# A gated linear attention and RWKV-7 layer in two phases: the second phase's four instruction lists in another order

## The chip, the cores and the metric

One core of one Trainium2 chip runs one program. The metric is the time of one execution in microseconds on the device; three executions were timed and the median counts.

## The reference, cut to what matters

One layer reads 4096 prompt tokens (one stream) and 128 sample tokens (8 streams of 16 tokens, with states carried in). Its mixer has two head groups. The first, gated linear attention, is the kernel's first phase. The second, RWKV-7, is its second phase, together with the output projection:

```
h = rms_norm(x, norm_pre);  p = h @ w_in
xm = p_shift + rwkv_mu * (prev - p_shift)          # prev: the row of the token before
r, kr, vr, wd, ad = split(xm)                      # 512, 512, 512, 64, 64 columns
w = exp(-0.6065 * sigmoid(w0 + tanh(wd) @ w_up))   # decay, low rank
a = sigmoid(a0 + ad @ a_up)                        # rate, low rank
kk = kr * k_k / norm(kr * k_k);  kr = kr * (1 + (a - 1) * k_a)
S_t = S_{t-1} (diag(w_t) - kk_t^T (a_t * kk_t)) + v_t^T k_t ;  y_t = S_t r_t     # 8 heads of 64
y = group_norm(y) * ln_w + ln_b                    # mean and variance over the 64 of a head
o_rwkv = (y + sum(r * kr * r_k) * vr) * silu(z_r)
x = x + rms_norm([o_gla, o_rwkv] @ w_out, norm_post)
```

All of it is float32. The order of the work does not enter into it.

## The kernel before, in words

**Blocks, tiles and chunks.** Block 0 holds the 128 sample tokens, and blocks 1 to 16 hold 256 prompt tokens each. A block is cut in tiles of 128 tokens (two of them, block 0 has one) for everything after the recurrence, and in chunks of 64 tokens (four of them, block 0 has two) for the recurrence. Within a chunk the recurrence is solved by a triangular inverse, so the state is only touched once in a chunk.

**The lists.** In the second phase each engine has one list for a *body*, which is one pass over a block: `PE_BODY` (TensorE), `ACT_BODY` (ScalarE), `DVE_BODY` (VectorE), `POOL_BODY` (GpSimd) and `SP_BODY` (the queue that issues DMAs). `body_jobs` goes through a list from left to right for b = 0 to 17 and hands out jobs; each engine runs its own jobs strictly in that order. Between engines there are only semaphores. A word is a job, its number after the colon is a chunk or a tile, `*3` is three times, and a dash in front means the block before. `out` marks a point; at the points of the last bodies the jobs of the output projection are put in.

**Three streams run in one body.** For block b+2 the projection is made: 39 *pieces* on TensorE, `x12` three times and `x4`, `x6`, `x0`, `x2`, `x8`, `x10` six times each, every piece 8 matmuls of 128x256. After a round, ScalarE (`taken`, L2028 and L2031) and VectorE (`mixed`, L2265 and L2271) make the token shift. The low-rank rounds are `lwa0` and `lwa2` (L1744, `rank`); ScalarE takes them with `tanh` (L2054), and VectorE makes the running decay from both halves of `lw` with `decay` (one L2279 and four scans L2282). `gamma` (L2093, L2096) needs `decay`. `squares`, `kn`, `clamp`, `rnorm` (L2078 to L2083), `unit` (L2299), `k_prime` (L2306, L2307), `beta` (L2320) and `a` (L2337) make the operands, and `xs` (L1762) multiplies them. `strict`, the blocks' way through memory, `invert` on GpSimd and `inverse_back` make the inverse, and VectorE turns it with `td` (L2381).

For the chunks of block b the recurrence runs, k = 0 to 3: `meet:k` (L1893, products with the state), `scores:k+1` (L1809), `inner:k+1` (L1838), `unknowns:k` (L1906), `turn:k+1` (L1820, L1824), `advance:k` (L1915, L1932, and L1876 which reads the state), `solve:k+1` (L1849), `join:k+1` (L1862). On the other engines: `zc` (L2405), `masked` (L2373), `even` and `keep_w` (L2421, L2389), `next` (L2430, L2432, the new state), `join_o` (L2397); `odd` (L2104), `turned` (L2124), `z1` (L2132), `join_e` (L2137), `keep_y` (L2116).

For the tiles, after the recurrence, there is the group norm: `centre` (L1953), `centred` (L2144, L2145), `variance` (L1961), `deviation` (L2149 to L2153), `normed` (L2455), `affine` (L2159, four instructions), `gated` (L2461, L2464), `high` (L2166) and `low` (L2468). Tile index 0 stands for the last tile of block b-1, and 1 for the first tile of block b.

**What waits for what, around the change.** `scores(q)` waits for `turned`, `z1`, `join_e` and `join_o` of chunk q-1. `inner(q)` waits for `masked` of chunk q and for `td` of its block. `meet(q)` waits for `next` and `keep_y` of chunk q-1. `xs` waits for `a`, and `next(q)` waits for the end of `advance(q)`. TensorE's rounds share four accumulator banks in turn, in the order in which the list names them, and a round may begin when the reader of the round four places ahead of it is done.

**The end.** From body 15 on there are no pieces any more; their places (all but those of `x12`) are filled with units of the output projection (L1717 too, 128x512), 12 to a tile, 396 in all. What is left of them after body 17 runs as one stretch.

Of the kernel before, what the change touches and what calls it, by code (L numbers as in the profile page):

```python
# [306 lines left out]
def gla_phase(nc, t, c):  # L307
# [739 lines left out]


PE_BODY = """
    meet:0 scores:1 centre:0 x12*3 inner:1 unknowns:0 turn:1 -bs x4*2 out x4 advance:0 solve:1 join:1 x4*3 lwa0  # L1050
    meet:1 scores:2 out lwa2 variance:0 x6*2 inner:2 unknowns:1 turn:2 x6*2 out x6*2 advance:1 solve:2 join:2
    x0*4 meet:2 out scores:3 x0*2 kn inner:3 unknowns:2 turn:3 x2*4 out x2 advance:2 solve:3 join:3 x2 centre:1
    x8*2 meet:3 scores:4 out x8*4 inner:4 unknowns:3 turn:4 xs variance:1 out x10*2 advance:3 solve:4 join:4
    x10*4 out
""".split()
ACT_BODY = """
    -taken:x10 -load_h centred:0 taken:x12 odd:0 turned:1 tanh_w out z1:1 join_e:1 keep_y:0 taken:x4 tanh:lw0
    out tanh:la0 squares:0 tanh:lw2 tanh:la2 deviation:0 odd:1 out turned:2 k_factor taken:x6 z1:2 keep_y:1
    join_e:2 affine:0 squares:2 out gamma taken:x0 odd:2 turned:3 high:0 rnorm:0 out rnorm:1 z1:3 join_e:3
    keep_y:2 taken:x2 centred:1 out taken:x8 odd:3 turned:4 out deviation:1 affine:1 z1:4 join_e:4 keep_y:3  # L1060
    high:1 out
""".split()
DVE_BODY = """
    zc:0 masked:1 -mixed:x10 -low:1 even:0 keep_w:1 mixed:x12 -bonus:0 out -r -bonus:1 next:0 join_o:1 mixed:x4
    out masked:2 zc:1 decay out even:1 keep_w:2 normed:0 next:1 mixed:x6 join_o:2 gated:0 out masked:3 zc:2
    clamp:0 even:2 mixed:x0 keep_w:3 clamp:1 low:0 out unit:0 unit:1 next:2 join_o:3 k_prime mixed:x2 out
    -td masked:4 zc:3 beta a mixed:x8 strict:0 out strict:1 even:3 keep_w:4 normed:1 rkk next:3 join_o:4 gated:1
    kappa out
""".split()
POOL_BODY = "-invert".split()  # L1070
SP_BODY = """
    -put_m:1 out -bonus_out out out out get_gate:0 out put_m:0 -inverse_back out out blocks_out blocks_in
    get_gate:1 out
""".split()
NPOINT = 8
# [1503 lines left out]
```

## Time and profile before

| | us |
|---|---|
| three executions | 2423.08, 2428.59, 2432.05 |
| median | 2428.59 |
| profiled execution, its own time | 2425.59 |
| its span | 2423.9 |

TensorE (PE) is busy for 95% of the span, ScalarE (ACT) for 60%, VectorE (DVE) for 51% and GpSimd (POOL) for 24%. The first phase ends at about 955 us; the bodies of the second phase run from about 1045 us to about 2140 us, and what follows is the rest of the output projection. Times in rows are counted from the start of the span. A row of a timeline has start, duration, engine, line, operation, what it writes from what, its shape and count, and in brackets the idle time of the engine before it with what ended it.

### The profile page before, as it was taken

The numbers are of one execution on the slowest core, as the hardware profiler recorded it, in microseconds if no ns is written. First come the engines' busy times: TensorE is split into PE (matmuls) and PEld (weight loads), VectorE is DVE, ScalarE is ACT, GpSimd is POOL, SyncE is SP. The second block draws the span as 40 slices with busy tenths as digits, with TensorE's granted clock in tenths as the row PEclk, the third lists the DMA queues.
The fourth block names the chain that finished last, engine by engine and source line by source line (L and its number), as shares of the span: only waits on it lengthen the run. The fifth ranks groups of instructions, "written<-read, shape, count | busy, mean of one in ns | idle before, by whom it ended". The sixth has DMA issues, their size and how long they took to land. (4 is left out here: it accounts for less than half of the span.)

```text
span 2423.9 us, 71744 instructions
## 1 busy us (share of the span) xinstructions
PE 2303.8 (95%) x31098; PEld 1730.8 (71%) x31098; DVE 1236.7 (51%) x2321; ACT 1452.9 (60%) x2821; POOL 571.9 (24%) x1069
## 2 busy tenths in 40 slices
PE   3999999999999997889999999999999998999998
PEld 3777777777777776767888888888888775544443
DVE  4423344343333333457777777777777676432222
ACT  6556666665666644644676767777777674553233
POOL 0000000000000000255455555555545555000000
PEclk9999999999999998999999999999999999999999
DMA  5222222222211111122222222222222234344443
GB/s 202 70 76 72 67 71 72 72 67 71 98 58 53 53 62 48 37 56 58 72 75 74 75 74 75 73 67 75 68 60 60 71 99 145 113 150 156 157 150 128
DMA packets 196858, 204.73 MB, mean 84 GB/s; under 512 B 108736, under 2 KB 152064, under 8 KB 192192
## 3 DMA queue, kind: packets, MB, share of 16 engines
q1 hardware_dynamic: 194384, 184.41, 25.3%
q10 hardware_dynamic: 2160, 15.73, 1.7%
q8 instruction: 247, 4.05, 0.7%
q14 instruction: 67, 0.55, 0.1%
HBM read 119.81 MB, written 80.28 MB: 83 GB/s over the span
## 5 line engine op out<-in xcount | busy, mean ns | idle before, releaser
L1717 PE MATMUL r_d<-h,w_hi 128*128 128x256 f16 (+1 forms) x3536 | 589.1, 272 | 6.2 <-PEq L316 5.4
L627 PE MATMUL d<-h,w_hi 128*128 128x256 f16 (+1 forms) x3264 | 525.7, 270 | 4.1 <-DVE h L907 4.1
L1717 PE MATMUL r_d<-h,w_lo 128*128 128x256 f16 (+1 forms) x1768 | 477.2, 272 | 0.0
L627 PE MATMUL d<-h,w_lo 128*128 128x256 f16 (+1 forms) x1632 | 436.2, 270 | 0.0
L1717 PEld LDWEIGHTS r_d<-h,w_hi 128*128 128x128 f16 x3536 | 337.8, 99 | 77.5 <-issue 33.9
L1678 POOL TENSOR_TENSOR r_inv_tmp<-r_inv 64x30 f32<-64x30 f32 (+14 forms) x480 | 261.3, 544 | 454.5 <-DMA r_inv<-scratch_blocks 418.1
L627 PEld LDWEIGHTS d<-h,w_hi 128*128 128x128 f16 x3264 | 314.9, 98 | 54.1 <-issue 12.4
L1717 PE MATMUL r_d<-w_hi,r_ops 128*128 128x512 f16 x1056 | 316.9, 382 | 3.9 <-DMA r_ops<-scratch_mr 3.9
L1680 POOL TENSOR_TENSOR r_inv<-r_inv,r_inv_tmp 64x30 f32<-64x30 f32 (+14 forms) x480 | 279.2, 582 | 37.6
L1622 POOL MEMSET r_run_s<- 128x128 f16 x1 | 0.2, 206 | 956.1 <-POOLq L316 956.1
L1717 PE MATMUL r_d<-w_lo,r_ops 128*128 128x512 f16 x528 | 201.6, 382 | 0.0
L1717 PEld LDWEIGHTS r_d<-w_hi,r_ops 128*128 128x128 f16 x1056 | 103.0, 98 | 129.7 <-issue 11.0
L1717 PEld LDWEIGHTS r_d<-h,w_lo 128*128 128x128 f16 x1768 | 175.1, 99 | 21.0 <-issue 2.6
L627 PEld LDWEIGHTS d<-h,w_lo 128*128 128x128 f16 x1632 | 160.2, 98 | 17.4
L627 PE MATMUL d<-w_hi,h 128*128 128x512 f16 x528 | 157.0, 379 | 0.0
L2185 ACT ACTIVATE r_xb<-r_d 128x512 f32<-128x512 f32 x66 | 39.4, 597 | 187.7 <-PE r_d L1717 187.6
L2265 DVE SCALAR_TENSOR_TENSOR r_ops<-r_d,r_sc,r_praw 128x256 f32<-128x256 f32 (+3 forms) x238 | 106.3, 470 | 64.9 <-ACT r_praw L2031 62.1
L2484 DVE TENSOR_TENSOR r_ops<-r_d,h 128x512 f32<-128x512 f32 x66 | 45.6, 691 | 179.7 <-ACT r_xb L2185 179.7
L2028 ACT ACTIVATE r_praw<-r_carry 128x2 f32<-128x2 f32 (+1 forms) x112 | 22.5, 201 | 140.1 <-PE r_d L1717 140.0
L627 PE MATMUL d<-w_lo,h 128*128 128x512 f16 x264 | 100.1, 379 | 0.0
L627 PEld LDWEIGHTS d<-w_hi,h 128*128 128x128 f16 x528 | 51.7, 98 | 63.5 <-issue 8.6
L1717 PEld LDWEIGHTS r_d<-w_lo,r_ops 128*128 128x128 f16 x528 | 51.9, 98 | 62.5 <-issue 1.7
(272 smaller groups left out, 4148.8 us busy)
## 6 DMA issues: line engine op xcount, KB each, us to landing
h<-in_x SPq DMA_DIRECT2D x33, 512.0 KB, 4.4
r_ops<-in_x SPq DMA_DIRECT2D x33, 512.0 KB, 4.3
out_y<-r_ops SPq DMA_DIRECT2D x33, 512.0 KB, 2.9
scratch_hT<-h SPq DMA_DIRECT2D x16, 1024.0 KB, 6.8
h<-scratch_hT ACTq DMA_DIRECT2D x15, 1024.0 KB, 6.8
scratch_mg<-m_hl SPq DMA_DIRECT2D x33, 256.0 KB, 2.0
r_zr<-scratch_zr SPq DMA_DIRECT2D x33, 256.0 KB, 3.4
r_bon<-scratch_bonus SPq DMA_DIRECT2D x33, 256.0 KB, 4.6
```

What stands on the lines that cost most here:

```text
L627: mm = pe.matmul(out, lhs(k, a, w), rhs(k, a, w), start=(n == 0), stop=(n == len(terms) - 1))
L1622: pool.memset(m[:, :], v).then_inc(*set_ok.up(0))
L1678: step(pool.tensor_tensor(tmp, inv[0:n, 0:u, u:u + 1].to_broadcast([n, u, w]), inv[0:n, u:u + 1, u + 1:32].to_broadcast([n, u, w]), ALU.mult))
L1680: step(pool.tensor_tensor(inv[0:n, 0:u, u + 1:32], inv[0:n, 0:u, u + 1:32], tmp, ALU.add))
L1717: mm = pe.matmul(out, lhs(k, a, w), rhs(k, a, w), start=(m == 0), stop=(m == 3 * KT - 1))
L2028: act.activation(praw[:, x % 2, 0:ng, 0], carry[:, g0:g0 + ng], ACT.Copy)
L2185: act.activation(o_junk[h], bank_of(("out", tile, h))[:, :], ACT.Square, accum_out=st[:, tile % 2, h:h + 1]).then_inc(*os_ok.up(tile))
L2265: dve.scalar_tensor_tensor(out=out[to, g], in0=pair[rows, g], scalar=par_s("mu1", g0 + g)[rows], in1=before[rows, g], op0=ALU.mult, op1=AL ...
L2484: dve.tensor_tensor(t_c[:, h * 512:(h + 1) * 512], bank_of(("out", tile, h))[:, :], npost[:, h * 512:(h + 1) * 512], ALU.mult).then_inc(*o ...
```

## The change

Only the lists are changed; every job is still there, once.

```diff
 PE_BODY = """
-    meet:0 scores:1 centre:0 x12*3 inner:1 unknowns:0 turn:1 -bs x4*2 out x4 advance:0 solve:1 join:1 x4*3 lwa0
-    meet:1 scores:2 out lwa2 variance:0 x6*2 inner:2 unknowns:1 turn:2 x6*2 out x6*2 advance:1 solve:2 join:2
-    x0*4 meet:2 out scores:3 x0*2 kn inner:3 unknowns:2 turn:3 x2*4 out x2 advance:2 solve:3 join:3 x2 centre:1
-    x8*2 meet:3 scores:4 out x8*4 inner:4 unknowns:3 turn:4 xs variance:1 out x10*2 advance:3 solve:4 join:4
+    meet:0 scores:1 centre:0 x12*3 inner:1 unknowns:0 turn:1 -bs variance:0 x4 out x4 advance:0 solve:1 join:1
+    x4*4 meet:1 scores:2 out lwa0 x6*3 inner:2 unknowns:1 turn:2 x6*3 out lwa2 advance:1 solve:2 join:2 x0*4
+    meet:2 out scores:3 x0*2 kn inner:3 unknowns:2 turn:3 x2*3 out x2 advance:2 solve:3 join:3 x2*2 centre:1
+    x8*2 meet:3 out scores:4 x8*4 inner:4 unknowns:3 turn:4 xs variance:1 out x10*2 advance:3 solve:4 join:4
     x10*4 out
 """.split()
 ACT_BODY = """
-    -taken:x10 -load_h centred:0 taken:x12 odd:0 turned:1 tanh_w out z1:1 join_e:1 keep_y:0 taken:x4 tanh:lw0
-    out tanh:la0 squares:0 tanh:lw2 tanh:la2 deviation:0 odd:1 out turned:2 k_factor taken:x6 z1:2 keep_y:1
-    join_e:2 affine:0 squares:2 out gamma taken:x0 odd:2 turned:3 high:0 rnorm:0 out rnorm:1 z1:3 join_e:3
-    keep_y:2 taken:x2 centred:1 out taken:x8 odd:3 turned:4 out deviation:1 affine:1 z1:4 join_e:4 keep_y:3
-    high:1 out
+    -taken:x10 -load_h centred:0 taken:x12 odd:0 turned:1 tanh_w out deviation:0 z1:1 join_e:1 keep_y:0 affine:0
+    taken:x4 out high:0 tanh:lw0 tanh:la0 odd:1 squares:0 turned:2 out taken:x6 tanh:lw2 tanh:la2 z1:2 join_e:2
+    keep_y:1 squares:2 k_factor out gamma taken:x0 odd:2 turned:3 rnorm:0 out rnorm:1 z1:3 join_e:3 keep_y:2
+    taken:x2 centred:1 out taken:x8 odd:3 turned:4 out deviation:1 affine:1 z1:4 join_e:4 keep_y:3 high:1 out
 """.split()
 DVE_BODY = """
-    zc:0 masked:1 -mixed:x10 -low:1 even:0 keep_w:1 mixed:x12 -bonus:0 out -r -bonus:1 next:0 join_o:1 mixed:x4
-    out masked:2 zc:1 decay out even:1 keep_w:2 normed:0 next:1 mixed:x6 join_o:2 gated:0 out masked:3 zc:2
-    clamp:0 even:2 mixed:x0 keep_w:3 clamp:1 low:0 out unit:0 unit:1 next:2 join_o:3 k_prime mixed:x2 out
-    -td masked:4 zc:3 beta a mixed:x8 strict:0 out strict:1 even:3 keep_w:4 normed:1 rkk next:3 join_o:4 gated:1
+    zc:0 masked:1 -mixed:x10 -low:1 mixed:x12 even:0 keep_w:1 -bonus:0 -bonus:1 out -r next:0 normed:0 join_o:1
+    gated:0 out zc:1 masked:2 mixed:x4 low:0 even:1 keep_w:2 out mixed:x6 next:1 decay out join_o:2 zc:2
+    masked:3 clamp:0 even:2 mixed:x0 keep_w:3 clamp:1 out unit:0 unit:1 next:2 join_o:3 k_prime mixed:x2 out
+    zc:3 masked:4 beta -td a even:3 mixed:x8 out strict:0 strict:1 keep_w:4 normed:1 rkk next:3 join_o:4 gated:1
     kappa out
 """.split()
 POOL_BODY = "-invert".split()
 SP_BODY = """
-    -put_m:1 out -bonus_out out out out get_gate:0 out put_m:0 -inverse_back out out blocks_out blocks_in
+    -put_m:1 out -bonus_out out get_gate:0 put_m:0 out out out -inverse_back out out blocks_out blocks_in
     get_gate:1 out
 """.split()
```

## Rows read from the trace of the kernel before

**Rows 1.** The page: busy time and share of each engine.
```profile
PE 2303.8 (95%) x31098; PEld 1730.8 (71%) x31098; DVE 1236.7 (51%) x2321; ACT 1452.9 (60%) x2821; POOL 571.9 (24%) x1069
```
**Rows 2.** Who waited for whom, TensorE, 1125 to 1920 us: total, times, longest.
```profile
PE r_d L1762 <- DVE r_ops L2337: 8.7, 12, 0.7
```
**Rows 3.** Timeline, TensorE: `solve:2`, `scores:3`; `inner:4`, `xs`; the next body's `inner:1`, `-bs`.
```profile
1462.58 0.41 PE L1849 MATMUL r_AB<-r_bu,h 64*64 64x64 f32 x16
...
1467.18 1.06 PE L1809 MATMUL r_AB<-r_ops 64*64 64x128 f32 x32
...
1487.16 0.43 PE L1838 MATMUL r_EO<-r_TD,h 64*64 64x32 f32 x16
...
1489.29 1.16 PE L1762 MATMUL r_d<-r_ops 64*64 64x64 f32 x64 [0.73 <-DVE r_ops L2337]
...
1503.29 0.43 PE L1838 MATMUL r_EO<-r_TD,h 64*64 64x32 f32 x16
...
1504.51 0.41 PE L1783 MATMUL r_d<-r_scr,r_rk_sum 64*64 64x256 f32 x4
```
**Rows 4.** Timeline, VectorE: `decay`, then the start of `next:1`.
```profile
1455.18 0.69 DVE L2279 TENSOR_SCALAR r_gin<-r_gin 128x1024 f32<-128x1024 f32 x1 [1.00 <-ACT r_gin L2054]
1455.91 3.93 DVE L2282 TENSOR_TENSOR_SCAN r_gin<-r_run_p,r_gin 128x256 f32<-128x256 f16 x4
...
1462.90 0.42 DVE L2430 TENSOR_TENSOR r_S<-r_EO,r_S 128x256 f32<-128x256 f32 x1 [1.96 <-PE r_EO L1876]
```
**Rows 5.** Timeline, VectorE: `unit:1`, `next:2`, `join_o:3`, `td`, `masked:4`, `a`.
```profile
1479.40 0.88 DVE L2299 SCALAR_TENSOR_TENSOR r_ops<-r_ops,r_sc 128x256 f32<-128x256 f32 x2 [1.81 <-ACT r_ops L2083]
1480.19 0.41 DVE L2430 TENSOR_TENSOR r_S<-r_EO,r_S 128x256 f32<-128x256 f32 x1
...
1481.10 0.29 DVE L2397 COPY r_TT<-r_AB 32x128 f32<-32x128 f32 x1
...
1484.67 0.70 DVE L2381 STREAM_TRANSPOSE r_TD<-r_T 128x512 f32<-128x512 f32 x1
1485.30 1.25 DVE L2373 TENSOR_TENSOR h<-r_AB,r_mask_p 128x512 f32<-128x512 f32 x2
...
1487.93 1.21 DVE L2337 TENSOR_TENSOR r_ops<-r_ops,r_gam 128x1024 f32<-128x1024 f32 x1
```
**Rows 6.** Timeline, ScalarE: `high:0`, which stands between `turned:3` and `rnorm:0`.
```profile
1473.34 0.63 ACT L2166 ACTIVATE r_m_hl<-r_yT 128x512 f16<-128x512 f32 x1
```
**Rows 7.** Timeline, ScalarE: `deviation:0` up to `odd:1`, and `affine:0`.
```profile
1455.89 1.28 ACT L2149 ACT_TABLE_LOAD   x1
...
1458.49 0.38 ACT L2104 ACTIVATE r_bu<-r_EO 64x256 f32<-64x256 f32 x1
...
1464.16 1.63 ACT L2159 ACTIVATE r_yT<-r_yT,r_lnb_s,r_sc 128x128 f32<-128x128 f32 x4
```
**Rows 8.** Timeline, several engines: bodies 13, 14 (output weights, L2473) and 15.
```profile
1929.63 0.71 DVE L2381 STREAM_TRANSPOSE r_TD<-r_T 128x512 f32<-128x512 f32 x1 [1.90 <-DMA r_T<-scratch_inverse]
...
1931.99 0.43 PE L1838 MATMUL r_EO<-r_TD,h 64*64 64x32 f32 x16 [1.79 <-DVE r_Zc L2405]
...
1977.24 1.64 DVE L2473 SCALAR_TENSOR_TENSOR w_lo<-h,w_hi 128x512 f16<-128x512 f32 x2 [0.39 <-ACT w_hi L2174]
...
2015.66 0.43 PE L1838 MATMUL r_EO<-r_TD,h 64*64 64x32 f32 x16 [1.81 <-DVE h L2373]
...
2022.27 0.65 PE L1717 MATMUL r_d<-w_hi,r_ops 128*128 128x512 f16 x2 [3.85 <-DMA r_ops<-scratch_mr]
...
2051.90 0.43 PE L1838 MATMUL r_EO<-r_TD,h 64*64 64x32 f32 x16 [2.74 <-DVE r_Zc L2405]
```
**Rows 9.** Stretches: PE, PEld, DVE, ACT, POOL busy (instructions), PEclk, DMA share, GB/s.
```profile
1933.90:1937.30 3.40, 3.04 (x66) 2.44 (x67) 2.78 (x7) 1.94 (x3) 0.00 (x0) 0.50 0.02 5
2015.70:2019.10 3.40, 2.45 (x96) 1.81 (x96) 3.15 (x8) 2.35 (x5) 2.93 (x7) 1.00 1.06 343
2053.40:2056.80 3.40, 3.40 (x9) 1.21 (x8) 1.35 (x3) 2.16 (x5) 0.12 (x1) 0.50 0.79 274
```

## The prediction

> **What bounds the kernel now.** I read the page first. It has TensorE busy for 95% of the span, with no other engine near it [rows 1]. The order of TensorE's own list and the waits in it are therefore all that another order can alter. Next come the waits of TensorE over the steady bodies (1125 to 1920 us, some twelve bodies and a half). Only one dependency counts there: `xs` waits for VectorE's `a`, twelve times, 0.7 us each [rows 2]. The timeline of one such body shows the place. `inner:4` begins at 1487.16 and `xs` at 1489.29, 2.13 us later, with 0.73 us idle; the same four jobs take 1504.51 - 1503.29 = 1.22 us in the next body, where nothing waits [rows 3]. So the steady wait costs 2.13 - 1.22 = 0.91 us a body. Larger waits stand at the end of body 13 and in body 15 [rows 8].
>
> **What TensorE's new list costs by itself: nothing.** It has the same jobs, and `x` pieces stand in 13 stretches in a body before and after, so the switches between the two kinds of matmul are as many. Only new or removed waits count.
>
> **Term A: a new wait at `scores:3`.** `scores:3` waits for `join_o:2`. In the new VectorE list `join_o:2` stands behind `next:1` and `decay`; before, `decay` lay in an earlier quarter. `next:1` can only begin when `advance:1` is through, so `decay` can't begin early either. On VectorE, counted from the end of `advance:1` (the start of `solve:2`, 1462.58):
> - the end reaches `next:1` after 1462.90 - 1462.58 = 0.32 us [rows 3, 4];
> - `next` takes 1481.10 - 1480.19 = 0.91 us [rows 5];
> - `decay` takes from 1455.18 to 1455.91 + 3.93 = 1459.84, 4.66 us [rows 4];
> - `join_o` takes 0.29 us [rows 5];
> - an end on VectorE reaches TensorE 0.15 us later (`a` ends at 1487.93 + 1.21 = 1489.14, `xs` begins at 1489.29) [rows 3, 5].
>
> That is 6.33 us, or 6.28 us if `decay` overlaps its neighbours by 0.05 us. TensorE has `solve:2`, `join:2`, four pieces and `meet:2` before `scores:3`, and the kernel before has them in exactly this order: 1467.18 - 1462.58 = 4.60 us [rows 3]. So TensorE stands for 6.28 - 4.60 = 1.68 us in each body that has a `decay` and a full recurrence, bodies 1 to 14: 14 x 1.68 = 23.5 us. Behind `join_o:2` in VectorE's queue are `zc:2` and `masked:3`; they are wanted by `inner:3` and `unknowns:2`, and two pieces and `kn` lie in between, so the wait isn't paid twice. Behind `scores:3` on TensorE everything moves back together; `clamp`, `rnorm` and `unit` hang on it too. Bounds: 1.4 us if the handovers are shorter, 1.95 us if `next` is slowed by a neighbour. That the instructions get their time in the new place too is assumed; ScalarE gives the `tanh:lw2` that `decay` needs in time, since it is two jobs behind `taken:x6` and the end of `advance:1` comes 1.4 us after `lwa2`.
>
> The row has the four scans at 3.93 us, 0.98 us each [rows 4]. The Trainium skill ("DVE: opcode table, instruction layouts, handler registers and perf-mode slots", 6. Datapath and trigger behaviour) says that the built-in scan runs at half throughput, which with the 0.96 GHz of its page "VectorE: DVE Perf Modes" gives an estimate of 0.53 us for 256 columns. By that figure the four would take 2.1 us and the wait would be gone, which is the first rival's case below. The trace has nearly twice as much.
>
> **Term B: the wait at the body's end gets shorter.** `xs` comes late because of a chain without slack: `turned:3`, `high:0`, `rnorm:0`, `rnorm:1` on ScalarE, then `unit:1` (which waits for it, 1.81 us) and an unbroken run on VectorE up to `a` [rows 5, 6]. The new list has `high:0` two quarters earlier. It took 0.63 us [rows 6], so the run on VectorE begins 0.63 us sooner. From the place of `td` (1484.67 - 0.63 = 1484.04) the new order is `zc`, `masked`, `beta`, `td`, `a`. The first three take 1487.93 - 1485.30 = 2.63 us, so `td` begins at 1486.67 and ends at 1487.37 [rows 5]. `inner:4` needs it, and with 0.15 us of handover goes at 1487.52 in place of 1487.16. `xs` is then wanted at 1488.74 and `a` is there at 1488.66. So `xs` begins 0.55 us earlier than before: -0.55 x 14 = -7.7 us. Bounds: 0 and -0.91 a body.
>
> **The first quarter.** `variance:0` now stands there, and ScalarE gets `deviation:0` (1458.49 - 1455.89 = 2.60 us) before `z1:1`, and `affine:0` (1.63 us) after `keep_y:0` [rows 7]. Laid out from `meet:0`, `tanh_w` is through at 8.7 us, `deviation:0` at 11.3, and `join:1` ends at 11.7, so `z1:1` isn't delayed. `gated:0` ends at 16.0 and `zc:1` follows, wanted by `unknowns:1` at 20.6. These are zero, covered by the pieces. With the cover gone, half of `deviation` would show, 1.3 us a body, and that stays in the range. The low-rank rounds stand behind six pieces each; the banks they claim had their readers done at least 4 us before by the same layout: zero. SP's `get_gate:0` and `put_m:0` come one quarter and more earlier, with nothing urgent behind them; `inverse_back` waits for GpSimd anyway: zero, at most 0.5 us either way.
>
> **Terms at single places.**
> - Body 13: `td` waited 1.90 us for its DMA and `inner:4` lost 1.79 us [rows 8]. With `td` two jobs later, and each body longer by term A, the DMA is in time: -1.8 us. The granted clock fell to 0.50 of full, the lower of its two levels (1.2 of 2.4 GHz), for 3.4 us right behind it [rows 9]; half of that, -1.7 us, goes too.
> - Body 0, two chunks only: `decay` begins behind `lwa2` there. Between 0 and +1.7 us, I take +1.0.
> - Body 14: the splitting of the output weights (a pair took 1.64 us [rows 8]) is put at the points, and point 3 now lies between `decay` and `join_o:2`. +1.6 us, bounds 0 and +3.
> - Body 15: TensorE waits 3.85 us for the first rows of the output projection. `variance:0` now goes before that, so about 1.0 us of it is filled: -1.0. `inner:3` lost 2.74 us behind `gated:0` and the first tile's last step [rows 8]; `gated:0` is out of the way now, but `join_o:2` stands behind the same step. I take -1.0, bounds -2.7 and +1. The clock fell behind that wait too (0.50 for 3.4 us [rows 9]); -1.7 if the wait is shorter.
>
> **Sum.** 23.5 - 7.7 - 3.5 + 1.0 + 1.6 - 3.7 = +11.2 us. The profiled execution took 2425.59 us and would take 2436.8. The median of the runs is 3.0 us above it, so the median should come out at 2428.59 + 11.2 = 2439.8; I say 2440.
>
> **Rivals.**
> - *The wait at `scores:3` isn't there* (the scans take less in the new place, or VectorE gets to them sooner than I think). Then terms A, body 0 and body 14 fall out, and -7.7 - 3.5 - 3.7 = -14.9 us is left: 2414. For it: the lists were laid against each other with some costs, and a wait of 1.7 us in each body is a large one to leave. That says nothing of the trace, though, and the trace has a scan of 0.98 us in every body and a fixed order on both engines. Chance 0.17.
> - *The clock falls behind each new wait*, slower than before and by more than my sum. It decides where an idle stretch of 1.7 us is enough to bring the granted clock down. For it: behind 1.79 us in body 13 it went to 0.50 [rows 8, 9]. Against it: behind 1.81 us at 2015.66 it stayed at 1.00 [rows 8, 9], and the twelve waits of 0.7 us left no trace. Each fall costs half of 3.4 us: 14 x 1.7 = 23.8 us on top, 2464. The Trainium skill ("TensorE: Matmul & The Clock Gate", A second HAM failure mode: psum-queue depth-cycling) tells of frequent short idles that make the clock swing, and by it this would be the case. Chance 0.13, with a few falls by chance inside the forecast's own range.
>
> **How the numbers follow.** The forecast holds 0.70, with its own range 2430 to 2450. A difference of 0.5% is 12.1 us and is about what a measurement of this kernel can tell from no change; the three runs alone span 9 us. The forecast's +11.2 lies just inside, so of its 0.70 I give 0.45 to no change and 0.25 to slower. The first rival gives 0.12 to faster and 0.05 to no change; the second gives 0.13 to slower. Together: faster 0.12, same 0.50, slower 0.38. The range goes from 2421 to 2457: beneath it lies most of the first rival, above it most of the second, and it takes in term A between 1.4 and 1.95 us (-4 and +4), term B between its bounds (-5 and +8) and the single places.
>
> **What would show it.** In the waits of TensorE a row with `scores` (L1809), released by VectorE's `join_o` (L2397), 14 or 15 times at about 1.7 us, is term A. `xs` (L1762) should hardly wait any more, and `inner` (L1838) should wait some 0.3 us for `td` (L2381). The stretch at half clock at 1934 us should be gone. If L1809 has no wait, the first rival holds. If the stretches behind each `scores:3` have a clock of 0.5, it is the second. I am wrong altogether if TensorE waits in the first quarter, for `z1`, `join_o:1` or `zc:1`.

## The result, and the profile after

| | before | after |
|---|---|---|
| median, us | 2429.5 (4 runs, 2423.08 to 2432.05) | 2455.34 (4 runs, 2453.5 to 2457.7) |
| profiled execution, its span, us | 2425.59, 2423.9 | 2453.5, 2451.7 |

The ratio is 1.012, with a 95% interval from 1.01 to 1.0139: the kernel is slower. The forecast was 2440 us and its range 2421 to 2457; the difference came out at +25.8 us (+27.8 between the two profiled spans) where +11.2 was said. Two of the six executions of the third experiment below were slow ones (2689 and 9682 us, at a granted clock of 0.85 and 0.22) and are left out of its numbers. Line numbers behind the lists are one lower than before: `scores` is L1808, `inner` L1837, `xs` L1761, `join_o` L2396, `decay` L2278 and L2281, `td` L2380, `a` L2336, `masked` L2372.

The page of after, busy time of each engine (against [rows 1]):

```profile
PE 2313.5 (94%) x31098; PEld 1737.8 (71%) x31098; DVE 1228.0 (50%) x2321; ACT 1477.4 (60%) x2835; POOL 568.5 (23%) x1069
```

TensorE has as many instructions and is busy 9.7 us longer; the other 18 us by which the span grew are idle. Which waits these are is told by the view of who waited for whom, TensorE, 1125 to 1940 us (total, times, longest), to be read against [rows 2]:

```profile
PE r_AB L1808 <- DVE r_TT L2396: 19.5, 13, 1.8
PE r_EO L1837 <- issue: 4.3, 12, 0.4
PE r_AB L1819 <- issue: 2.5, 1, 2.5
PE r_d L1761 <- issue: 2.3, 2, 1.5
```

The row of `xs` and `a` is gone, and the row of term A stands in its place, `scores` behind `join_o`: twelve waits of 1.47 to 1.81 us in bodies 2 to 13, and one of 0.40 us in body 1. The second row is `inner:4`, for which the view names no engine ("issue"); in the timelines below `td` ends 0.10 us before it begins.

TensorE in one steady body: `solve:2`, `meet:2`, `scores:3`, then `inner:4` and `xs` (against [rows 3]).

```profile
1473.66 0.41 PE L1848 MATMUL r_AB<-r_bu,h 64*64 64x64 f32 x16
...
1477.97 0.46 PE L1892 MATMUL r_EO<-r_S,r_ops 64*64 64x64 f32 x16
1479.92 1.10 PE L1808 MATMUL r_AB<-r_ops 64*64 64x128 f32 x32 [1.49 <-DVE r_TT L2396]
...
1500.41 0.44 PE L1837 MATMUL r_EO<-r_TD,h 64*64 64x32 f32 x16 [0.38 <-issue]
...
1501.60 1.14 PE L1761 MATMUL r_d<-r_ops 64*64 64x64 f32 x64
```

VectorE beside it: `next:1`, `decay`, `join_o:2`, and later `masked:4`, `beta`, `td`, `a` (against [rows 4, 5]).

```profile
1473.97 0.42 DVE L2429 TENSOR_TENSOR r_S<-r_EO,r_S 128x256 f32<-128x256 f32 x1 [0.72 <-PE r_EO L1875]
1474.43 0.42 DVE L2431 TENSOR_TENSOR r_S<-r_S,r_gL 128x256 f32<-128x256 f32 x1
1474.78 1.05 DVE L2278 TENSOR_SCALAR r_gin<-r_gin 128x1024 f32<-128x1024 f32 x1
1475.86 3.60 DVE L2281 TENSOR_TENSOR_SCAN r_gin<-r_run_p,r_gin 128x256 f32<-128x256 f16 x4
1479.49 0.29 DVE L2396 COPY r_TT<-r_AB 32x128 f32<-32x128 f32 x1
...
1497.28 1.28 DVE L2372 TENSOR_TENSOR h<-r_AB,r_mask_p 128x512 f32<-128x512 f32 x2
1498.47 1.21 DVE L2319 SCALAR_TENSOR_TENSOR r_ops<-r_ops,r_gin 128x1024 f32<-128x1024 f32 x1
1499.61 0.70 DVE L2380 STREAM_TRANSPOSE r_TD<-r_T 128x512 f32<-128x512 f32 x1
1500.23 1.18 DVE L2336 TENSOR_TENSOR r_ops<-r_ops,r_gam 128x1024 f32<-128x1024 f32 x1
```

`decay` fills VectorE from 1474.78 to 1479.46 without a gap, `join_o:2` follows, and TensorE stands. From `solve:2` to `scores:3` it is 1479.92 - 1473.66 = 6.26 us, where it was 4.60 [rows 3].

Where the 27.8 us of the spans are, counted from `xs` to `xs`: 1.5 us lie ahead of body 0's `xs` (1103.1 against 1101.6; 1.7 of them are there one `xs` earlier, before body 0 begins), 20.2 us in bodies 1 to 14, and 6.1 us behind the last `xs` (428.3 against 422.1). The two stretches of the fourteen bodies, before and then after (length, then busy time of PE, PEld, DVE, ACT, POOL, the granted clock, DMA):

```profile
1101.60:2001.70 900.10, 878.84 (x18182) 729.84 (x18183) 648.70 (x1203) 628.33 (x1371) 480.09 (x854) 1.00 0.27 72
```
```profile
1103.10:2023.40 920.30, 880.30 (x18199) 730.27 (x18191) 639.56 (x1205) 653.77 (x1384) 478.02 (x854) 0.99 0.26 71
```

TensorE is busy for 1.5 us more in them and idle for 18.7 us more. A body that nothing disturbs takes 64.3 us where it took 62.9; the mean of bodies 2 to 12, some of which hold a further short wait in either kernel, is 64.8 against 63.5. Body 14 is one that is disturbed. Waits of TensorE from 1930 to 2023.4 us, and the split of the output weights on VectorE in it, followed by `td`:

```profile
PE r_AB L1808 <- DVE r_TT L2396: 4.9, 2, 3.2
PE r_EO L1837 <- issue: 3.0, 2, 2.6
```
```profile
2016.53 1.28 DVE L2472 SCALAR_TENSOR_TENSOR w_lo<-h,w_hi 128x512 f16<-128x512 f32 x2
...
2020.40 0.70 DVE L2380 STREAM_TRANSPOSE r_TD<-r_T 128x512 f32<-128x512 f32 x1
```

Its `scores:3` waits 3.2 us, and its `inner:4` 2.6 us, since another pair of the output weights goes ahead of `zc:3`, `masked:4`, `beta` and `td`. That second wait is no loss against the kernel before, whose body 14 waited as long at the same place, at `inner:4` and at `xs`:

```profile
1999.46 0.43 PE L1838 MATMUL r_EO<-r_TD,h 64*64 64x32 f32 x16 [1.90 <-DVE r_Zc L2405]
...
2001.72 0.47 PE L1762 MATMUL r_d<-r_ops 64*64 64x64 f32 x17 [0.83 <-DVE r_ops L2337]
```

Behind the last `xs`, in bodies 15 to 17, the waits of TensorE from 2023.4 to 2170 us:

```profile
PE r_EO L1837 <- DVE h L2372: 5.4, 3, 2.1
PE r_d L1716 <- DVE w_lo L2472: 2.4, 1, 2.4
PE r_d L1716 <- DMA r_ops<-scratch_mr: 2.2, 1, 2.2
PE r_AB L1808 <- DVE r_TT L2396: 1.8, 2, 1.0
PE r_d L1960 <- ACT r_yT L2144: 1.7, 1, 1.7
```

They and one of 0.6 us come to 14.1 us. Before, the waits behind the last `xs` came to 13.4 us, those of 1.81, 3.85 and 2.74 us in [rows 8] among them: the places are others, the sum is nearly the same. What differs is the granted clock behind them (columns as in [rows 9]):

```profile
2020.60:2024.00 3.40, 2.80 (x105) 2.83 (x108) 3.15 (x6) 0.69 (x2) 0.00 (x0) 0.50 0.02 5
2037.70:2041.10 3.40, 3.39 (x92) 2.94 (x96) 2.69 (x7) 1.28 (x3) 2.93 (x7) 0.50 1.03 342
2044.50:2047.90 3.40, 3.06 (x8) 1.02 (x8) 2.59 (x3) 0.90 (x2) 3.17 (x4) 0.50 1.01 340
2058.20:2061.60 3.40, 3.40 (x9) 1.22 (x8) 2.43 (x4) 0.00 (x0) 3.09 (x5) 0.50 0.22 69
2106.00:2109.40 3.40, 3.40 (x82) 2.64 (x79) 1.09 (x3) 1.51 (x4) 0.00 (x0) 0.50 0.24 88
```

The first begins in the wait ahead of body 14's `inner:4`, the other four lie behind the last `xs`, where there were two before. With what the first reaches over, that is 7.4 us more at half clock. If half of that is lost, it is 3.7 of the 6.1 us (an estimate); 0.7 are waits, and the rest stands in no wait.

### The profile page after: what moved, and what is told of

Its sections match the earlier page's. It is cut to its first block, busy times and chain, and to the rows that moved or that the text cites. A ratio compares the mean times of both kernels' runs of the same rounds, so it can differ in the third digit from the quotient of the medians.

```text
span 2451.7 us, 71758 instructions
## 1 busy us (share of the span) xinstructions
PE 2313.5 (94%) x31098; PEld 1737.8 (71%) x31098; DVE 1228.0 (50%) x2321; ACT 1477.4 (60%) x2835; POOL 568.5 (23%) x1069
## 3 DMA queue, kind: packets, MB, share of 16 engines
q10 hardware_dynamic: 2160, 15.73, 1.7%
## 4 chain that ended last, share of the span: by engine, by line
PE 50%; DVE 5%; ACT 3%; issue 2%; DMA 0%; DVEq 0%; SPq 0%; ACTq 0%
PE r_d L1716 33%; PE r_AB L1808 2%; PE r_EO L1914 2%; DVE r_gin L2281 2%; PE r_d L1743 1%; PE r_AB L1819 1%; PE r_d L1960 1%; PE r_d L1782 1%; PE r_EO L1931 1%; PE r_EO L1875 1%; PE r_EO L1837 1%; PE r_EO L1892 1%; PE r_EO L1905 1%; PE r_AB L1861 1%; PE r_d L1761 1%
## 5 line engine op out<-in xcount | busy, mean ns | idle before, releaser
L1716 PE MATMUL r_d<-h,w_hi 128*128 128x256 f16 (+1 forms) x3536 | 589.4, 273 | 8.5 <-PEq L316 5.4
L1716 PE MATMUL r_d<-h,w_lo 128*128 128x256 f16 (+1 forms) x1768 | 478.9, 273 | 0.0
L1716 PEld LDWEIGHTS r_d<-h,w_hi 128*128 128x128 f16 x3536 | 338.8, 99 | 79.5 <-issue 31.3
L1677 POOL TENSOR_TENSOR r_inv_tmp<-r_inv 64x30 f32<-64x30 f32 (+14 forms) x480 | 268.3, 559 | 478.6 <-DMA r_inv<-scratch_blocks 442.2
L1716 PE MATMUL r_d<-w_hi,r_ops 128*128 128x512 f16 x1056 | 317.3, 382 | 6.3 <-DMA r_ops<-scratch_mr 3.9
L1679 POOL TENSOR_TENSOR r_inv<-r_inv,r_inv_tmp 64x30 f32<-64x30 f32 (+14 forms) x480 | 271.5, 566 | 37.6
L1716 PE MATMUL r_d<-w_lo,r_ops 128*128 128x512 f16 x528 | 201.3, 381 | 0.0
L1716 PEld LDWEIGHTS r_d<-w_hi,r_ops 128*128 128x128 f16 x1056 | 102.9, 98 | 132.7 <-issue 13.7
L1716 PEld LDWEIGHTS r_d<-h,w_lo 128*128 128x128 f16 x1768 | 175.8, 99 | 21.9 <-issue 2.7
L627 PEld LDWEIGHTS d<-w_hi,h 128*128 128x128 f16 x528 | 51.7, 98 | 63.5 <-issue 8.6
L1716 PEld LDWEIGHTS r_d<-w_lo,r_ops 128*128 128x128 f16 x528 | 51.9, 98 | 62.3 <-issue 1.6
```

The costliest lines, as they stand in the source:

```text
L627: mm = pe.matmul(out, lhs(k, a, w), rhs(k, a, w), start=(n == 0), stop=(n == len(terms) - 1))
L1677: step(pool.tensor_tensor(tmp, inv[0:n, 0:u, u:u + 1].to_broadcast([n, u, w]), inv[0:n, u:u + 1, u + 1:32].to_broadcast([n, u, w]), ALU.mult))
L1679: step(pool.tensor_tensor(inv[0:n, 0:u, u + 1:32], inv[0:n, 0:u, u + 1:32], tmp, ALU.add))
L1716: mm = pe.matmul(out, lhs(k, a, w), rhs(k, a, w), start=(m == 0), stop=(m == 3 * KT - 1))
```

## The experiments

Nine kernels ran: five are edits of the kernel after, three of the kernel before, one takes from both. All ratios are to the kernel before on the same chip: its median was 2425.99 us beside the first four, 2428.38 beside the next four and 2425.82 beside the last. Across chips the ratios are compared and not the times.

**`join_o:2` ahead of `decay`.** Term A alone undone.

```diff
 DVE_BODY (after)
-    ... mixed:x6 next:1 decay out join_o:2 zc:2
+    ... mixed:x6 next:1 join_o:2 decay out zc:2
```

> The kernel after, with join_o:2 ahead of decay in VectorE's list and nothing else changed. Theory (the wait at scores:3 is decay standing ahead of join_o:2, 1.5 us idle and 1.75 us by starts in each of bodies 1 to 14): the row L1808 <- L2396 vanishes from TensorE's waits, the body falls from 64.3 to 62.5 us, and the time is 2455 - 14 x 1.75 = about 2431. Rival (the longer stretches, the early variance or a lower clock cost the time, and the wait is only where it shows): another wait takes its place, and the time stays above 2445.

It took 2427.62 us (11 runs), ratio 1.0001 [0.9991, 1.0012]. So all of the 1.2% hangs on the place of `decay` (27.7 us between the medians); between the two profiled executions 23.9 us of it are in bodies 1 to 14 (920.3 to 896.4 us). That the kernel is then level with before is a balance: these bodies are 3.7 us shorter than before, and what lies ahead of them and behind them is 1.4 and 5.9 us longer. The steady body takes 62.7 us (after: 64.3), and the row of L1808 is gone. What is left of the end wait, timelines of VectorE and TensorE and the waits from 1125 to 1925 us:

```profile
1490.52 0.70 DVE L2380 STREAM_TRANSPOSE r_TD<-r_T 128x512 f32<-128x512 f32 x1
```
```profile
1491.33 0.43 PE L1837 MATMUL r_EO<-r_TD,h 64*64 64x32 f32 x16 [0.67 <-issue]
```
```profile
PE r_EO L1837 <- issue: 7.6, 12, 0.7
```

`td` ends at 1491.22 and `inner:4` goes 0.11 us later. Twelve waits of up to 0.67 us stand where twelve of 0.73 us stood [rows 2, 3]: term B is a wait put in another place. It is shorter in the kernel after, 0.38 us, where `scores:3` has held TensorE back already.

**The same wait put into the kernel before.** This makes term A in the old lists.

```diff
 DVE_BODY (before)
-    out masked:2 zc:1 decay out even:1 keep_w:2 normed:0 next:1 mixed:x6 join_o:2
+    out masked:2 zc:1 out even:1 keep_w:2 normed:0 next:1 mixed:x6 decay join_o:2
```

> The kernel before, with decay moved behind next:1 and mixed:x6, ahead of join_o:2; nothing else. By the sum of my prediction, 0.32 + 0.91 + 1.27 for mixed:x6 + 4.6 + 0.3 + 0.15 - 4.6 = 2.95 us are lost at scores:3 in each of 14 bodies: 2430 + 41 = 2471. Rival (the granted clock falls behind each such wait): 14 x 1.7 = 24 us more, 2495. Rival (decay is not what scores:3 waits for): about 2430.

It took 2470.65 us, ratio 1.0176 [1.0157, 1.0196]. The waits from 1125 to 1925 us:

```profile
PE r_AB L1809 <- DVE r_TT L2397: 24.4, 12, 2.3
PE r_d L1762 <- DVE r_ops L2337: 8.5, 12, 0.7
```

The waits are 2.03 to 2.31 us in bodies 2 to 13, and `xs` still waits 0.7 us in each body: the chain to `a` starts at `turned:3` and moves back with TensorE, so the two waits add up. The stretches behind three of the waits, of six where the clock fell:

```profile
1223.40:1226.80 3.40, 3.40 (x20) 2.19 (x22) 1.85 (x4) 0.67 (x3) 2.85 (x8) 0.50 0.40 120
1356.50:1359.90 3.40, 3.40 (x19) 2.20 (x16) 2.22 (x4) 0.75 (x2) 2.80 (x8) 0.50 0.36 98
1889.00:1892.40 3.40, 3.40 (x20) 2.19 (x16) 2.05 (x4) 0.83 (x2) 2.93 (x7) 0.50 0.38 106
```

Behind six of these twelve waits the clock falls, and a body with a fall takes some 68 us where the others take 65.5. The total is near the expectation's (44.7 us above the kernel before, 41 were said), but partly by luck: from `solve:2` to `scores:3` it is 6.9 us in the mean, so each wait costs 2.3 us and not 2.95, and the falls, which only the rival had, fill up the rest.

**The old lists for bodies 15 to 17.**

```diff
+PE_END, ACT_END, DVE_END, SP_END = ...    # the four lists of the kernel before
 def body_jobs(...)
+    if b > LAST - 2:
+        table = END.get(id(table), table)
```

> The kernel after up to body 14, and the lists of the kernel before in bodies 15 to 17. Theory: the stretch behind the last xs, which is 6 us longer in the trace after than before (428.3 against 422.2), takes what it took before: 2455 - 6 = 2449. Rival (that stretch is late because of what bodies 1 to 14 left behind, or by chance of the clock): within 2 us of 2455.

It took 2450.1 us (median of four executions), ratio 1.0092 [1.0072, 1.0111], against after's 1.012 [1.01, 1.0139]: less, as the theory has it, but the two intervals overlap. In the profiled execution the part behind the last `xs` went from 428.3 to 422.5 us, as long as in the kernel before (422.1), though bodies 1 to 14 have the lists of the kernel after. So the order there takes part in the cost. That the new order always costs 6 us there isn't shown: two kernels below keep it but for one edit each (`high:0` back in its place; `td` ahead of `beta`), wait about 13 us behind the last `xs` at the places of the kernel after, and end in 421.9 and 422.6 us in their profiled executions, each the fastest of its kernel. They spend 6 and 9.5 us there at half clock, where the kernel after spends 14.2. How the 6.1 us divide between the order and the clock of one execution stays open.

**`high:0` back in its old place, on top of the first.** This asks what its move was worth.

```diff
 ACT_BODY (as after, join_o:2 first; DVE low:0 and SP put_m:0 moved with it)
-    taken:x4 out high:0 tanh:lw0 ... turned:3 rnorm:0 out rnorm:1
+    taken:x4 out tanh:lw0 ... turned:3 high:0 rnorm:0 out rnorm:1
```

> As the first one, with high:0 back between turned:3 and rnorm:0, low:0 behind clamp:1, and put_m:0 just ahead of inverse_back. Theory (high:0 lies on the chain to td and a): its 0.63 us show in full at inner:4 or xs in each body, 14 x 0.63 = 9 us above the first one, about 2440. Rival (the chain has slack, or is set by something else): within 2 us of the first one.

It took 2436.78 us, ratio 1.0042 [1.0026, 1.0058], 9.2 us more than without this edit, where 14 x 0.63 = 8.8 us was laid out for `high:0` on that chain [rows 6]. In the profiled executions bodies 1 to 14 are 7.7 us longer. The waits from 1125 to 1925 us:

```profile
PE r_EO L1837 <- issue: 14.0, 12, 1.2
```

1.2 us in place of 0.7. So the step "the run on VectorE begins 0.63 us sooner" held. `td` behind `beta` takes most of it back: the first experiment, with both, still waits 0.63 us in the mean where the kernel before waited 0.73.

**`td` ahead of `beta`, on top of the first.**

```diff
 DVE_BODY (as after, join_o:2 first)
-    zc:3 masked:4 beta -td a
+    zc:3 masked:4 -td beta a
```

> As e1_join_first, with td ahead of beta in VectorE's list. Theory (inner:4 waits for td, 0.6 us in each body of e1_join_first): td is through 1.1 us sooner and inner:4 goes at once; xs then waits for a, 0.3 us. So 0.3 to 0.4 us a body come back, 14 x 0.35 = 5 us: 2427.6 - 5 = 2423. Rival (that wait is for masked:4 or zc:3 and not for td): within 1 us of e1_join_first.

It took 2423.79 us, ratio 0.9991 [0.9976, 1.0006], against 1.0001 [0.9991, 1.0012] of the first experiment: the intervals overlap, so a gain isn't shown. The waits from 1125 to 1925 us:

```profile
PE r_d L1761 <- DVE r_ops L2336: 5.4, 12, 0.5
```

The wait goes back to `xs` and is 0.45 us. Of the 5.4 us by which bodies 1 to 14 are shorter, 3.6 are in body 1 (72.7 to 69.1 us); a steady body takes 62.7 us in both. So the 2423 us of the expectation are met by number only: the gain of 0.3 to 0.4 us in each body isn't there. What is shown is that `inner:4` had waited for `td`.

**One table load in place of two.** The chain that ends in `a` holds two loads of the same table set on ScalarE; here the second is left out. The kernel before otherwise.

```diff
 def rnorm(arg):
-    act.preload_act_table_set(LN_SET)
+    if k == 0:
+        act.preload_act_table_set(LN_SET)
```

> The kernel before, with one load of the activation table for rnorm:0 and rnorm:1 together in place of one for each; the second is a load of the set that is there already. Theory (turned:3, high:0, rnorm:0, rnorm:1, unit:1 up to a is one chain without slack, which sets xs): its 1.28 us cover the whole 0.91 us that xs loses in each body, and the row L1762 <- L2337 goes from TensorE's waits: 2426 - 14 x 0.91 = 2413. Rival (the chain on ScalarE has slack against TensorE): within 2 us of 2426.

It took 2409.42 us, ratio 0.9922 [0.99, 0.9943], the fastest kernel but for the next, with which it is level. That is 19 us less than before, where the expectation had 13. ScalarE in the kernel before:

```profile
1473.99 1.28 ACT L2078 ACT_TABLE_LOAD   x1
1475.28 0.63 ACT L2081 ACTIVATE r_ops<-r_ops 128x512 f32<-128x512 f32 x1
1475.95 0.72 ACT L2083 ACTIVATE r_ops<-r_ops,consts 128x512 f32<-128x512 f32 x1
1476.69 1.28 ACT L2078 ACT_TABLE_LOAD   x1
```

With the second load gone, the whole chain is 1.28 us earlier. That is more than the 0.73 us that `xs` had waited. From 1125 to 1920 us TensorE waits for no other engine any more. Bodies 2 to 12 take 62.0 to 63.2 us, 1.1 us less in the mean, and bodies 1 to 14 together 883.7 us where they took 900.1.

**Both together: one load, `join_o:2` first, the old lists in bodies 15 to 17.**

```diff
 rnorm: one load;  DVE_BODY: next:1 join_o:2 decay out;  bodies 15 to 17 from the lists of before
```

> The kernel after, with join_o:2 ahead of decay up to body 14, the lists of before in bodies 15 to 17, and one table load for the two rnorm. Theory: no wait is left in a steady body (62.7 falls to 62.0 us, 14 x 0.7 = 10 us under e1_join_first), and the end gives 4 us: about 2414, level with e7_one_load, so that the change's longer stretches and early variance are worth nothing by themselves. Rival (they are worth something once the waits are gone): under 2410.

It took 2408.36 us, ratio 0.992 [0.9899, 0.994], level with the kernel above. The rival said under 2410, but the kernel above came out at 2409.42 itself, so that bound decides nothing; a steady body takes 62.0 us in both. Once the chain to `a` has room and `decay` lies behind `join_o:2`, no gain or loss by the new lists of bodies 0 to 14 shows, within intervals of some 5 us either way.

**The old list of the DMA queue in the kernel after.**

```diff
 SP_BODY (after)
-    -put_m:1 out -bonus_out out get_gate:0 put_m:0 out out out -inverse_back
+    -put_m:1 out -bonus_out out out out get_gate:0 out put_m:0 -inverse_back
```

> The kernel after with SP_BODY as it was before. One theory of the 4 us that the last bodies lose: SP's put_m:0 now stands ahead of the fetches of the output weights and waits there for low:0, so the weights come late; then 2455 - 4 = 2451, and the wait for w_lo in body 15 is gone. Rival (the lists of the other engines do it, or the clock): within 1.5 us of 2455.

It took 2456.72 us, ratio 1.0119 [1.0099, 1.0139]: no difference from after, and TensorE still waits 2.3 us for `w_lo`. The theory that the earlier `get_gate:0` and `put_m:0` carry a part of the cost has fallen; the prediction's zero for them holds.

**More of the output projection in bodies 16 and 17**, on the kernel with one load. The expectation calls the base wrongly a load "of the weights' sum of squares"; it is ScalarE's table load, as in "One table load in place of two" above.

```diff
 elif e + 2 > LAST and name in XROUNDS:
-    if name != "x12":
+    if name != "x12" or b >= LAST:
```

> The kernel before with one load of the weights' sum of squares in place of two (as e7_one_load), and in bodies 16 and 17 also the places of x12 given to the output's projection, so that masked:1 no longer stands right behind scores:1. Theory: the waits of TensorE of 1.8 us each at inner:1 in these two bodies go and nothing takes their place: 2409 - 3.6 = 2406 us, ratio to the kernel before 0.9907. Rival: the projection's steps come later in their chain and the time is given back at the end: within 1.5 us of 2409, ratio 0.992.

It took 2417.91 us (12 runs), ratio 0.9975 [0.996, 0.9989]: 0.5% (some 13 us) more than the kernel with one load by the ratios, and a miss for both expectations. In the profiled executions the part behind the last `xs` takes 433.5 us in place of 420.7, and TensorE's waits from 2000 to 2160 us come to 18.2 us in place of 6.4. Two of them, in bodies 16 and 17:

```profile
2111.48 1.87 PE L1961 MATMUL r_d<-r_y_sq,r_headmean 128*128 128x512 f32 x2 [1.94 <-DVE r_ops L2485]
2125.69 1.13 PE L1953 MATMUL r_d<-r_yT,r_centre 64*64 64x128 f32 x16 [4.64 <-DVE r_ops L2485]
```

L2485 is VectorE's reader of the projection's accumulator banks. With more projection rounds put in, `variance` and `centre` of the last tiles find their bank still unread. The places of `x12` were no free time: the rounds put there stand in the way of the tiles' own rounds.

## Why the prediction was wrong in its size

The direction and the main mechanism held; the sum was less than half of what came, and most of what it missed lies in the terms at single places. By its own steps:

- **Term A, right.** Predicted 1.68 us a body from VectorE's queue; measured 6.26 - 4.60 = 1.66 us in the body shown, 1.77 us in the mean of bodies 2 to 13, and without it 1.6 us of the steady body go. Body 1, which the sum counts too, lost only 0.6 us here. The layout of the queue is right in its sum (6.28 us laid out), in part because errors cancel: the scans took 3.60 us for 3.93 and `next` 0.81 for 0.91, while L2278 took 1.05 us where L2279 had 0.69.
- **Term B, mis-sized.** Predicted -0.55 us a body. Measured: `inner:4` comes 0.45 us late behind `td` (0.38 us of it idle) where 0.36 was laid out, so -0.46. The first experiment shows the weak point of the term: the place of `td` binds nearly as much as the chain to `a` did (0.67 against 0.73 us).
- **The two together.** 1.77 - 0.46 = 1.31 us against 1.13 predicted. An undisturbed body lost 1.4 us, the mean of bodies 2 to 12 1.3. Fourteen bodies at 1.4 us are 19.6 us, where 23.5 - 7.7 = 15.8 were said.
- **The terms at single places are the step that failed.** Body 0, body 13, body 14 and body 15 were put at 1.0 - 3.5 + 1.6 - 3.7 = -4.6 us. What lies outside the 19.6 us is 27.8 - 19.6 = +8.2 us: 1.5 ahead of body 0's `xs`, 0.6 in bodies 1 to 14 (for the most part body 1's +2.4 against body 13's -1.2), and 6.1 at the end. That is 12.8 of the 16.6 us by which the forecast was short of the profiled difference; 3.8 are the per-body terms.
  - *Body 0*, +1.0 us predicted. The wait isn't there: no `scores` waits for `join_o` before body 1, and body 0 takes 68.4 us where it took 68.7. What the trace has is earlier: 0.8 us ahead of the first `xs` of all, at 990 us, and 0.9 us between it and body 0.
  - *Body 15 and the end*, -3.7 us predicted, +6.1 measured; this is the largest miss. Each wait there was looked at by itself and taken as shortened. The DMA wait did shrink (3.85 to 2.2 us), but the output weights came up as a wait of their own (L1716 for `w_lo`, 2.4 us), `inner` has three of up to 2.1 us, and the sum didn't fall (13.4 to 14.1 us). The forecast also had one fall of the clock less there, and there were two more. With the old lists the end took 422.5 us; with the new ones it took 427.3 to 428.3 us in three profiled executions and 421.9 and 422.6 in two others. So that nothing was saved is shown, and how much of the 6.1 us is the order and how much the clock stays open.
  - *Body 14*, +1.6 us predicted. Its `scores:3` waits 3.2 us, and 1.68 + 1.6 = 3.3 was laid out, so this wait is right. The 2.6 us at `inner:4` stand where the kernel before had 1.90 + 0.83 us at `inner:4` and `xs`, and the body as a whole lost 1.6 us (67.5 to 69.1) where 1.13 + 1.6 = 2.7 were laid out.
  - *Body 13*, -3.5 us predicted. No wait for that DMA shows after, and the fall at 1933.90 is gone, yet body 13 is only 1.2 us nearer to a steady one (0.8 us above it, before 2.0), and body 14 is no nearer (4.8 and 4.6 us above).
  - *Body 1* wasn't in the sum. It took 73.0 us where it took 69.2: TensorE idles 2.53 us ahead of L1819 with no releaser in the profile, and the clock falls behind it. With `td` ahead of `beta` it takes 69.1. Why isn't settled.
- **The clock, at the end, not in the bodies.** The rival "falls behind each new wait" did not hold for the kernel after: one of its twelve long waits was followed by one (below). But four falls at the end in place of two make some 3.7 us by the estimate above, where the prediction had one less.
- **The first quarter and SP's list: zero, right.** No wait for `z1`, `join_o:1` or `zc:1` shows in the steady bodies, and the old SP list changes nothing.
- **The rival with fast scans** is out. The four scans took 3.60 us in the new place, after 3.93 [rows 4].

By the half-throughput rule that the prediction took from the Trainium skill ("DVE: opcode table, instruction layouts, handler registers and perf-mode slots", 6. Datapath and trigger behaviour) they would take 2.1 us, an estimate. The trace does not agree, with 0.90 us for one; the shortest four, in body 1 of the kernel after, took 0.66 to 0.73 us each, 2.8 in all.

## What to carry to other kernels

A wait on the bounding engine can be forecast by laying the other engine's queue against it from a common event: here it came out right to 0.1 us, and in the second experiment 0.6 us too long. Such a term repeats from body to body. The first and last rounds are another matter: a saving there should be counted only after asking which wait is next behind each one that goes, and the first and last bodies should be laid out as bodies of their own. Where the bounding engine waits at the end of a chain, look into the chain for work that need not be there, before its order is altered: leaving out one redundant table load of 1.28 us in each block was worth 19 us, more than any order of the lists tried here.

## What the runs showed of the hardware

**What the clock did behind TensorE's waits.** The wait at `scores:3` ahead of the one fall among the twelve long waits of the kernel after, then the stretch behind the wait of 1.49 us shown above and the one behind this:

```profile
1801.55 1.43 PE L1808 MATMUL r_AB<-r_ops 64*64 64x128 f32 x32 [1.81 <-DVE r_TT L2396]
```
```profile
1479.00:1482.40 3.40, 2.48 (x46) 2.19 (x47) 2.46 (x5) 3.36 (x4) 3.01 (x6) 1.00 0.00 0
1802.20:1805.60 3.40, 3.40 (x32) 2.28 (x22) 1.29 (x2) 1.54 (x3) 2.93 (x7) 0.50 0.02 5
```

The clock stayed at 1.00 behind 1.49 us, and behind all of the waits of 1.47 to 1.64 us. With 2.03 to 2.31 us in the second experiment it fell behind six of twelve, and not behind the longest ones. The same twelve waits in the profiled executions of the third experiment and of the one with the old SP list (1.46 to 2.00 us) were followed by one fall, behind 1.94 us, and by none. So a fall is more frequent behind 2 us than behind 1.5 us of idle in these places of this kernel, without a sharp bound that these runs show. A fall costs some 2 us: the one body with it takes 66.2 us against 64.3 in the kernel after, and 68 against 65.5 in the second experiment. The Trainium skill ("TensorE: Matmul & The Clock Gate", A second HAM failure mode: psum-queue depth-cycling) has frequent short idles make the clock swing; the second experiment's run agrees with it, the kernel after hardly does, with one fall behind twelve waits.

**A table load costs its time again even when its set is already there.** In the rows of the kernel with two loads, both take 1.28 us, with the same set and nothing but its own two activations between. The kernel after has 14 more of them than before (ACT x2835 against x2821 [rows 1]), since `deviation:0` now stands between two `tanh` jobs, ScalarE's view by lines:

```profile
L2053 ACT ACT_TABLE_LOAD x14 | 18.0, 1283 | 0.2
```

They make most of ScalarE's 24.5 us of added busy time, and no wait of TensorE for ScalarE shows in the steady bodies. A switch to another set costs the same in the kernel after, where a load follows the `tanh` of L2036, which ends at 1455.72:

```profile
1455.74 1.28 ACT L2148 ACT_TABLE_LOAD   x1
1457.03 0.66 ACT L2150 ACTIVATE r_d<-r_d,consts 128x512 f32<-128x512 f32 x1
```

The load begins 0.02 us after the activation before it, and the next one 0.01 us after the load. The Trainium skill ("ScalarE: Activation LUTs", What ACT_TABLE_LOAD costs) adds a drain of 1380 ns to each switch; the trace does not show it.
